# Neighbourhood attention outputs by features: values held in TensorE, divided probabilities moving, two heads on two column halves

## The chip, the cores and the metric

One core of one Trainium2 chip runs the whole program. The metric is the device time of one execution in microseconds (us), as a median over several runs; lower is better.

## What is computed

A trunk of two layers over 256 tokens of width 1024, all in float32. Each layer is a mixer, a cross attention and a gated convolutional feed-forward. The change touches the mixer, which joins three groups of heads: six mLSTM heads (384 columns), five heads of 2-D neighbourhood attention (320 columns) and five heads of gated linear attention (GLA, 320 columns). For the neighbourhood heads, head size 64, this is

```
s = einsum('brqhd,brkwhd->bhrqkw', qg, k_band) * (d ** -0.5) + bias
s = where(in_win, s, -inf)
p = softmax(s)                        # over all keys of a query
o = einsum('bhrqkw,brkwhd->brqhd', p, v_band)
...
mixed = concatenate([ml_out, na_out, gla_out], axis=-1)
return mixed @ w_out
```

The grid is 4 rows of 64 columns, so that every query sees all 4 rows; the window in the columns is a mask in `bias`. Hence p is, for each head, a full 256 x 256 matrix.

## The kernel before

Every engine runs an order written out by hand, and engines wait for each other on semaphores that count finished jobs. TensorE (PE) multiplies; ScalarE (ACT) and VectorE (DVE) empty its banks of PSUM. A product with weights is made of three matmuls in fp32r: the weights come by DMA as `raw`, ACT makes `whi`, their rounded high part (L1096), and DVE makes `wlo`, the rest (L1455); activations are split the same way (`yhi`, `ylo`). A unit of weights (xk0, xv0a, wo0b ...) can be used once its low part is made. `split_lo(unit)` in DVE's order makes all low parts up to that unit.

The neighbourhood stage is the loop `for hh in range(NAH + 2)`, once in each engine's code. Its jobs for head g are:

- `nas{g}` (L882): scores on PE, two heads together, at hh = 0, 2 and 4. DVE subtracts bias and keeps the extreme (L1624), ACT makes the exponential into `np_` and its row sums `nsum` (L1262). `np_` has two places, g modulo 2.
- `nat{g}` (L864): four turnings of `np_`, at hh = g + 1; ACT copies them to `npt` (L1249).
- `nao{g}` (L872): the outputs, at hh = g + 2. The turned probabilities are held (128 x 128) and 64 columns of values `nav` move. DVE takes the reciprocal of `nsum` (L1611) and multiplies the outputs by it into `tmb` (L1614).

In between PE has fill work: halves (24 matmuls) of the units xk0 to xk3 of the cross attention, two halves at hh = 1, 2 and 3 and one at hh = 4 and 5 in layer 0; in layer 1 one half of 24 at hh = 1, 2 and 3, then 18 matmuls and 6. DVE has other work in the loop too: the low parts of the weights, the sums of the mLSTM heads, the gated queries and keys of GLA (L1646, L1647, at hh = 2), their decayed form (L1655, at hh = 3) and the squares of the mLSTM heads (L1588, `head_squares`). After the loop PE turns GLA keys, `kt0` (L900), into bank 5 and goes on with GLA.

When all three groups of heads are in `tmb`, PE turns its eight blocks of 128 columns (16 turnings, L978, `mx`), ACT writes `yhi` (L1301), DVE writes `ylo` (L1710), and PE multiplies by the output weights, units wo0a, wo0b, wo1a and wo1b. Blocks 3 and 4 and the first half of block 5 belong to the neighbourhood heads.

Of the kernel before, what the change touches and what calls it, by code (L numbers as in the profile page):

```python
# [21 lines left out]
P = 128  # L22
# [90 lines left out]
def layer_events(l):  # L113
# [43 lines left out]
    for h in range(NAH + 2):  # L157
        if 1 <= h <= NAH:
            job(f"nat{h - 1}", 2 + (h - 1) % 2)
        if h >= 2:  # L160
            job(f"nao{h - 2}", 4 + (h - 2) % 2)
        if h < NAH and h % 2 == 0:
            for n in range(h, min(h + 2, NAH)):
                job(f"nas{n}", n % 2)
        if h == 0:
            tm("gg", (7, 6))
        for i in NA_FILL[l][h]:
            if i % 2:
                job(f"xk{i // 2}", (7, 6)[i // 2 % 2], f"xk{i // 2}")
# [48 lines left out]
def layer_drains(l):  # L218
# [15 lines left out]
    for h in range(NAH + 2):  # L234
# [5 lines left out]
        if h >= 2:  # L240
            v.append(f"nao{h - 2}")
        if h < NAH and h % 2 == 0:
            v += [f"nas{n}" for n in range(h, min(h + 2, NAH))]
    v += ["kt0", "kt1"]
# [47 lines left out]
def build(nc, a, out):  # L292
    with ExitStack() as ctx:
# [31 lines left out]

        fhi = sb("fhi", [P, 2, 2, T], F32R)
        flo = sb("flo", [P, 2, 2, T], F32R)
        sb("early_rest", [P, T])
        with ExitStack() as mixer:
# [5 lines left out]
            eg = mixer.enter_context(nc.sbuf_tensor("eg", [P, TT, GV], F32))  # L335

# [139 lines left out]
        np_ready = sem("np_ready")  # L476
        zb_ready = sem("zb_ready")
# [45 lines left out]
        def mixed_parts(k):  # L523

            lo, hi = k * P, k * P + P
            return [(slice(max(lo, a) - lo, min(hi, b) - lo), v)
                    for a, b, v in ((0, ML, forwards), (ML, ML + NA, backwards), (ML + NA, DM, forwards)) if max(lo, a) < min(hi, b)]
# [110 lines left out]
        def _(pe):  # L638
# [10 lines left out]
            for l in range(DEPTH):  # L649
# [64 lines left out]
                def tm_half(unit, half, names, n, group, fresh=False, tokens=(0, 1), ks=range(4)):  # L714
                    have((l, unit + half))
                    hi, lo = weights((l, unit + half), 4)
                    x = PAIR[group]
                    for t in tokens:
                        if half == "a":
                            free(names[t])  # L720
                        for k in ks:
                            kk = 4 * "ab".index(half) + k
                            if fresh and t == 0:
                                lo_is(pe, l, group, kk)
                            s = slice(t * P, t * P + P)
                            way = from_the_end if unit in ("xv1", "xw1") and t == TT - 1 and kk == KT - 1 else (lambda v: v)
                            last = split_mm(way(bank(names[t])[:, 0:n]), x[0][:, kk, s], x[1][:, kk, s],
                                            way(hi[:, k, :]), way(lo[:, k, :]), kk == 0, kk == KT - 1)
                        if (half == "b" or t == TT - 1) and k == 3:
# [127 lines left out]
                for hh in range(NAH + 2):  # L857
                    if 1 <= hh <= NAH:
                        g = hh - 1
                        pe.wait_ge(np_ready, NAH * l + g + 1)  # L860
                        free(f"nat{g}")
                        for t in range(TT):
                            for jt in range(TT):
                                last = nc.tensor.transpose(bank(f"nat{g}", TT, TT, P)[:, t, jt, :], np_[:, g % 2, t, jt * P:(jt + 1) * P], ident[:])  # L864
                        last.then_inc(te_done, 1)
# [194 lines left out]
        def _(act):  # L1060
# [44 lines left out]
            for l in range(DEPTH):  # L1105
# [140 lines left out]
                for hh in range(NAH + 2):  # L1246
                    if 1 <= hh <= NAH:
# [48 lines left out]
                for k in range(KT):  # L1296
                    is_filled(act, l, f"mx_{k % 4}")
                    if k >= 4:
                        lo_is(act, l, "mx", k - 4)
                    for r, v in mixed_parts(k):  # L1300
                        last = A(forwards(yhi[r, k, :]), v(turned_bank(l, "mx", k)[r, :]), ACT.Copy, scale=pcol[r, R_MG + k:R_MG + k + 1])  # L1301
                    last.then_inc(xhi_ready, 1)
# [115 lines left out]
        def _(dve):  # L1418
# [39 lines left out]
            for l in range(DEPTH):  # L1458
# [145 lines left out]

                for hh in range(NAH + 2):
                    if hh == 2:
                        dve.wait_ge(eb_ready, 2 * l + 2)
                    if hh >= 2:
                        g = hh - 2
                        dve.wait_ge(np_ready, NAH * l + g + 1)  # L1610
                        link(V.reciprocal(nsum[:, 2 * g:2 * g + 2], nsum[:, 2 * g:2 * g + 2]))  # L1611
                        is_filled(dve, l, f"nao{g}")
                        for t in range(TT):
                            last = ts(tmb[:, t, ML + g * DH:ML + (g + 1) * DH], bank(f"nao{g}")[:, t * DH:(t + 1) * DH],  # L1614
                                      nsum[:, 2 * g + t:2 * g + t + 1], None, ALU.mult)
                        drain(last)
# [10 lines left out]
                    if hh == 0:  # L1627
                        split_lo("ggb")
# [260 lines left out]
```

## Time and profile before

| | |
|---|---|
| median of 3 runs | 880.57 us |
| lowest, highest | 878.48, 882.46 us |
| profiled execution | 878.24 us |
| its span from first to last instruction | 876.3 us |
| PE, DVE, ACT busy | 861.8, 596.0, 496.1 us |
| granted TensorE clock, mean | 0.998 |

The busy times are of the same span, and engines work side by side, so that they do not add up. A share of 98% on PE says that most of the time is its work; it does not say what a wait in one stage would cost. Every time below is of the profiled execution.

### The profile page before, as it was taken

The numbers are of one execution on the slowest core, as the hardware profiler recorded it, in microseconds if no ns is written. First come the engines' busy times: TensorE is split into PE (matmuls) and PEld (weight loads), VectorE is DVE, ScalarE is ACT, GpSimd is POOL, SyncE is SP. The second block draws the span as 40 slices with busy tenths as digits, with TensorE's granted clock in tenths as the row PEclk, the third lists the DMA queues.
The fourth block names the chain that finished last, engine by engine and source line by source line (L and its number), as shares of the span: only waits on it lengthen the run. The fifth ranks groups of instructions, "written<-read, shape, count | busy, mean of one in ns | idle before, by whom it ended". The sixth has DMA issues, their size and how long they took to land.

```text
span 876.3 us, 14948 instructions
## 1 busy us (share of the span) xinstructions
PE 861.8 (98%) x6338; PEld 798.1 (91%) x6338; DVE 596.0 (68%) x820; ACT 496.1 (57%) x689; POOL 14.3 (2%) x35
## 2 busy tenths in 40 slices
PE   8999999999999999999999999999999899999997
PEld 8999998889889999999999999988898899999996
DVE  6887678757657666666577885887665666656655
ACT  7954663658647445445567546745755645445444
POOL 5000000000000000000000000000000000000000
PEclk9999999999999999999999999999999999999999
DMA  9735452364255555555448254335435365555541
GB/s 329 201 102 177 156 178 103 112 226 144 97 193 190 195 190 195 192 191 194 145 140 257 72 171 165 127 115 192 135 109 191 127 212 190 193 196 190 192 169 48
DMA packets 114665, 146.78 MB, mean 168 GB/s; under 512 B 10600, under 2 KB 94760, under 8 KB 114600
## 3 DMA queue, kind: packets, MB, share of 16 engines
q1 hardware_dynamic: 114456, 145.57, 49.7%
q8 instruction: 50, 0.82, 0.4%
q10 hardware_dynamic: 144, 0.26, 0.1%
q14 instruction: 15, 0.12, 0.0%
HBM read 144.77 MB, written 1.05 MB: 166 GB/s over the span
## 4 chain that ended last, share of the span: by engine, by line
PE 92%; ACT 3%; DVE 3%; issue 1%; DMA 0%; ACTq 0%; DVEq 0%
PE bank L665 26%; PE bank L666 25%; PE bank L667 25%; PE bank L706 4%; PE bank L743 2%; PE bank L832 2%; DVE wlo L1455 2%; PE bank L1017 2%; ACT whi L1096 1%; ACT yhi L1119 1%; PE bank L872 1%; PE bank L762 1%; PE bank L849 1%; DVE ylo L1710 1%; PE bank L882 1%
## 5 line engine op out<-in xcount | busy, mean ns | idle before, releaser
L1455 DVE TENSOR_TENSOR wlo<-raw,whi 128x2048 fp32r<-128x2048 f32 (+3 forms) x144 | 306.2, 2133 | 106.1 <-ACT whi L1096 105.2
L1096 ACT ACTIVATE whi<-raw 128x2048 fp32r<-128x2048 f32 (+3 forms) x144 | 257.4, 1793 | 53.5 <-PE bank L667 48.4
L665 PE MATMUL bank<-yhi,whi 128*128 128x256 f32 x704 | 195.1, 277 | 0.5 <-DVE ylo L1471 0.5
L666 PE MATMUL bank<-ylo,whi 128*128 128x256 f32 x704 | 194.6, 276 | 0.0
L667 PE MATMUL bank<-yhi,wlo 128*128 128x256 f32 x704 | 194.6, 276 | 0.0
L665 PEld LDWEIGHTS bank<-yhi,whi 128*128 128x128 f32 x704 | 132.2, 188 | 1.6 <-issue 0.7
L666 PEld LDWEIGHTS bank<-ylo,whi 128*128 128x128 f32 x704 | 132.2, 188 | 0.8
L667 PEld LDWEIGHTS bank<-yhi,wlo 128*128 128x128 f32 x704 | 132.2, 188 | 0.0
L665 PE MATMUL bank<-xhi,whi 128*128 128x256 f32 x320 | 91.4, 286 | 2.2 <-DVE wlo L1455 1.2
L665 PE MATMUL bank<-whi,xhi 128*128 128x512 f32 (+2 forms) x256 | 90.1, 352 | 0.0
L667 PE MATMUL bank<-xhi,wlo 128*128 128x256 f32 x320 | 88.9, 278 | 0.0
L666 PE MATMUL bank<-xlo,whi 128*128 128x256 f32 x320 | 88.8, 278 | 0.0
L667 PE MATMUL bank<-whi,xlo 128*128 128x512 f32 (+2 forms) x256 | 88.5, 346 | 0.0
L666 PE MATMUL bank<-wlo,xhi 128*128 128x512 f32 (+2 forms) x256 | 88.5, 346 | 0.0
L666 PE MATMUL bank<-wlo,fhi 128*128 128x512 f32 x176 | 69.0, 392 | 0.0
L665 PE MATMUL bank<-whi,fhi 128*128 128x512 f32 x176 | 68.9, 391 | 0.0
L667 PE MATMUL bank<-whi,flo 128*128 128x512 f32 x176 | 68.6, 390 | 0.0
L665 PEld LDWEIGHTS bank<-xhi,whi 128*128 128x128 f32 x320 | 60.3, 188 | 7.1 <-issue 5.2
L1395 ACT ACTIVATE arena<-bank,pcols 128x256 f32<-128x256 f32 x44 | 22.4, 561 | 67.1 <-PE bank L667 67.1
L667 PEld LDWEIGHTS bank<-xhi,wlo 128*128 128x128 f32 x320 | 60.1, 188 | 0.0
L666 PEld LDWEIGHTS bank<-xlo,whi 128*128 128x128 f32 x320 | 60.1, 188 | 0.0
L665 PEld LDWEIGHTS bank<-whi,xhi 128*128 128x128 f32 x256 | 48.1, 188 | 5.1 <-issue 1.3
(268 smaller groups left out, 1373.1 us busy)
## 6 DMA issues: line engine op xcount, KB each, us to landing
raw<-in_w_up SPq DMA_DIRECT2D x44, 1024.0 KB, 5.0
raw<-in_w_down SPq DMA_DIRECT2D x22, 1024.0 KB, 4.8
raw<-in_w_in SPq DMA_DIRECT2D x10, 1024.0 KB, 7.3
raw<-in_w_xk SPq DMA_DIRECT2D x8, 1024.0 KB, 5.1
raw<-in_w_xv SPq DMA_DIRECT2D x8, 1024.0 KB, 4.9
raw<-in_w_out SPq DMA_DIRECT2D x8, 1024.0 KB, 4.8
raw<-in_w_xq SPq DMA_DIRECT2D x8, 1024.0 KB, 5.7
raw<-in_w_xo SPq DMA_DIRECT2D x8, 1024.0 KB, 4.9
```

What stands on the lines that cost most here:

```text
L665: mm(o, s_hi, m_hi, start=first, stop=False, skip_group_check=True)
L666: mm(o, s_hi, m_lo, start=False, stop=False, skip_group_check=True)
L667: return mm(o, s_lo, m_hi, start=False, stop=last, skip_group_check=True)
L706: last = mm(bank(name, 2, T)[:, f, :], w[:, k, f * P:f * P + P], x[:, k, :], start=k + i + f == 0, stop=k == KT - 1 and i == 2, skip_group ...
L743: last = mm(bank(names[t])[:, 0:n], x[:, k, t * P:(t + 1) * P], w[:, k, :], start=k + i == 0, stop=False, skip_group_check=True)
L762: last = nc.tensor.transpose(turned_bank(l, group, k)[:, t * P:(t + 1) * P], tmb[:, t, k * P:(k + 1) * P], ident[:])
L832: last = mm(o[:, t, d, :], w[:, c:c + P], mv[:, jt, g, :], start=i == 0, stop=i == len(src) - 1)
L849: last = mm(bank(f"mls{hh + x}", TT, T)[:, jt, :], qk[r, 3 + j, jt * P:(jt + 1) * P], qk[r, j, :], start=True, stop=True)
L1017: last = mm(bank(f"xo_{hh}", 2, T)[:, f, :], xv[:, jt, hh * XD + f * P:hh * XD + (f + 1) * P], xpt[:, hh, jt, :], start=jt == 0, stop=jt == 1)
L1096: A(weight(whi, gu), raw[:, gu % RING, 0:SIZE[gu]], ACT.Copy).then_inc(hi_done, 1)
L1395: last = A(fy[:, p % 2, f, :], bank(f"fa{p}", 2, T)[:, f, :], ACT.Identity, scale=pcol[:, RA + RB_W + 22 + j:RA + RB_W + 23 + j], bias=pco ...
L1455: tt(weight(wlo, gu), raw[:, gu % RING, 0:SIZE[gu]], weight(whi, gu), ALU.subtract).then_inc(lo_done, 1)
```

## The change

PE now makes the outputs with the values held (128 tokens x 64 features of one head) and the turned probabilities of all 256 queries moving. Of a pair of heads, one writes partitions 0 to 63 and the other 64 to 127 of the same bank. The three groups (heads 0 and 1, 2 and 3, and 4) are made at hh = 3, 5 and 6. What comes out has features on the partitions, which is what the output product needs, so blocks 3, 4 and half of 5 are no longer turned: ACT writes their high part `yna_hi` straight from the bank, and DVE their low part `yna_lo` (`heads_lo`). The row sums can't be divided out of such outputs by a factor per partition, so DVE divides `np_` by them before PE turns it (`shares_of`), and PE's turning waits for that (`npn_ready`) instead of for the exponential. The output product starts with block 3.

```diff
     for h in range(NAH + 2):
+        if h in NA_OUT:
+            p = NA_OUT.index(h)
+            job(f"nao{p}", 4 + p % 2)
...
-        if h >= 2:
-            job(f"nao{h - 2}", 4 + (h - 2) % 2)
...
+NA_OUT = (3, 5, 6)
+NA_PAIRS = ((0, 1), (2, 3), (4,))
+NA_K = range(3, 6)
...
+        def mixed(k):
+
+            r = slice(64, P) if k == 5 else slice(0, P)
+            return (r,) + tuple(x[r] for x in operand("mx", k))
+
+        MIXED_K = (0, 1, 2, 5, 6, 7)
...
                 for hh in range(NAH + 2):
+                    if hh in NA_OUT:
+                        p = NA_OUT.index(hh)
+                        is_drained(pe, l, f"nat{NA_PAIRS[p][-1]}")
+                        free(f"nao{p}")
+                        for jt in range(TT):
+                            for g in NA_PAIRS[p]:
+                                r = slice(64 * (g % 2), 64 * (g % 2) + 64)
+                                last = mm(bank(f"nao{p}")[r, 0:T], nav[:, jt, g * DH:(g + 1) * DH], npt[:, g % 2, jt].rearrange("p a b -> p (a b)"),
+                                          start=jt == 0, stop=jt == 1, skip_group_check=True)
+                        last.then_inc(te_done, 1)
                     if 1 <= hh <= NAH:
                         g = hh - 1
-                        pe.wait_ge(np_ready, NAH * l + g + 1)
+                        pe.wait_ge(npn_ready, NAH * l + g + 1)
...
-                    if hh >= 2:
-                        g = hh - 2
-                        is_drained(pe, l, f"nat{g}")
-                        free(f"nao{g}")
-                        for t in range(TT):
-                            for jt in range(TT):
-                                last = mm(bank(f"nao{g}")[:, t * DH:(t + 1) * DH], npt[:, g % 2, t, jt, :],
-                                          nav[:, jt, g * DH:(g + 1) * DH], start=jt == 0, stop=jt == 1)
...
                     for k in (i, i + 4):
+                        if k not in MIXED_K:
+                            continue
...
-                for n in range(2):
-                    tm_unit(f"wo{n}", (f"wo{n}0", f"wo{n}1"), 512, "mx", n == 0)
+                tm_half("wo0", "a", ("wo00", "wo01"), 512, "mx", True, ks=(3,), first=3, ends=None)
+                tm_half("wo0", "a", ("wo00", "wo01"), 512, "mx", True, ks=(0, 1, 2), first=3, ends=2)
+                tm_half("wo0", "b", ("wo00", "wo01"), 512, "mx", True)
+                tm_unit("wo1", ("wo10", "wo11"), 512, "mx")
...
                 for hh in range(NAH + 2):
+                    if hh in NA_OUT:
+                        p = NA_OUT.index(hh)
+                        r = slice(0, 64 * len(NA_PAIRS[p]))
+                        is_filled(act, l, f"nao{p}")
+                        A(forwards(yna_hi[r, p, :]), backwards(bank(f"nao{p}")[r, 0:T]), ACT.Copy).then_inc(na_hi_ready, 1)
...
+                def shares_of(g):
+                    dve.wait_ge(np_ready, NAH * l + g + 1)
+                    link(V.reciprocal(nsum[:, 2 * g:2 * g + 2], nsum[:, 2 * g:2 * g + 2]))
+                    for t in range(TT):
+                        last = ts(np_[:, g % 2, t, :], np_[:, g % 2, t, :], nsum[:, 2 * g + t:2 * g + t + 1], None, ALU.mult)
+                    last.then_inc(npn_ready, 1)
+
+                def heads_lo(p):
+                    dve.wait_ge(na_hi_ready, 3 * l + p + 1)
+                    r = slice(0, 64 * len(NA_PAIRS[p]))
+                    drain(tt(forwards(yna_lo[r, p, :]), backwards(bank(f"nao{p}")[r, 0:T]), forwards(yna_hi[r, p, :]), ALU.subtract))
...
-                    if hh >= 2:
-                        g = hh - 2
-                        dve.wait_ge(np_ready, NAH * l + g + 1)
-                        link(V.reciprocal(nsum[:, 2 * g:2 * g + 2], nsum[:, 2 * g:2 * g + 2]))
-                        is_filled(dve, l, f"nao{g}")
...
                     if hh == 0:
                         split_lo("ggb")
+                        for g in NA_PAIRS[0]:
+                            shares_of(g)
...
                         if l == 0:
                             split_lo("xk2")
+                        for g in NA_PAIRS[1]:
+                            shares_of(g)
...
                         if l == 0:
                             split_lo("xk3")
+                        heads_lo(0)
...
                     if hh == 4:
                         split_lo("xv0a")
-                    if hh == 5 and l:
-                        head_squares(mlh, sq, 0, MLH)
+                        shares_of(4)
+                    if hh == 5:
+                        if l:
+                            head_squares(mlh, sq, 0, MLH)
+                        heads_lo(1)
...
+                heads_lo(2)
```

What moves is seen best in each engine's own order. First DVE, layer 1, at hh = 2, between the reductions of heads 2 and 3 and the decayed keys; this is before the change, where `wlo` is the low part of xk3:

```order
L1624 ISA nmax 128x1
L1455 TENSOR_TENSOR wlo<-raw,whi 128x2048
L1646 TENSOR_TENSOR arena<-gq,arena 128x512
L1647 TENSOR_TENSOR arena<-gk,arena 128x512
L1646 TENSOR_TENSOR arena<-gq,arena 128x512
L1647 TENSOR_TENSOR arena<-gk,arena 128x512
L1611 RECIPROCAL nsum<-nsum 128x2
L1614 TENSOR_SCALAR tmb<-bank,nsum 128x64 x2
L1655 TENSOR_TENSOR arena<-arena 128x512 x2
```

and the same place of the changed kernel:

```order
L1661 ISA nmax 128x1
L1489 TENSOR_TENSOR wlo<-raw,whi 128x2048
L1685 TENSOR_TENSOR arena<-gq,arena 128x512
L1686 TENSOR_TENSOR arena<-gk,arena 128x512
L1685 TENSOR_TENSOR arena<-gq,arena 128x512
L1686 TENSOR_TENSOR arena<-gk,arena 128x512
L1641 RECIPROCAL nsum<-nsum 128x2
L1643 TENSOR_SCALAR arena<-arena,nsum 128x256 x2
L1641 RECIPROCAL nsum<-nsum 128x2
L1643 TENSOR_SCALAR arena<-arena,nsum 128x256 x2
L1696 TENSOR_TENSOR arena<-arena 128x512 x2
```

The reciprocal at this place was for head 1's outputs; now those of heads 2 and 3 stand here, with the division of the probabilities (in `arena`), behind xk3's low part and the four products of GLA.

Second PE, layer 1, around head 2's turning, at hh = 3. Before, behind the last matmuls of xk2:

```order
L665 MATMUL bank<-xhi,whi 128x256
L666 MATMUL bank<-xlo,whi 128x256
L667 MATMUL bank<-xhi,wlo 128x256
L864 MATMUL bank<-ident,arena 128x128 x4
L872 MATMUL bank<-nav,arena 128x64 x4
```

and after:

```order
L684 MATMUL bank<-xhi,whi 128x256
L685 MATMUL bank<-xlo,whi 128x256
L686 MATMUL bank<-xhi,wlo 128x256
L890 MATMUL bank<-arena,nav 64x256 x4
L899 MATMUL bank<-ident,arena 128x128 x4
```

The outputs of heads 0 and 1 now stand ahead of head 2's turning (L899), where those of head 1 stood behind it.

Third DVE, layer 0, at hh = 4 and 5, behind head 4's reductions. Before:

```order
L1624 ISA nmax 128x1
L1588 TENSOR_TENSOR qk<-qk 128x768
L1589 TENSOR_REDUCE hs<-qk 128x12
L1455 TENSOR_TENSOR wlo<-raw,whi 128x2048
L1611 RECIPROCAL nsum<-nsum 128x2
L1614 TENSOR_SCALAR tmb<-bank,nsum 128x64 x2
```

and after:

```order
L1661 ISA nmax 128x1
L1622 TENSOR_TENSOR qk<-qk 128x768
L1623 TENSOR_REDUCE hs<-qk 128x12
L1489 TENSOR_TENSOR wlo<-raw,whi 128x2048
L1641 RECIPROCAL nsum<-nsum 128x2
L1643 TENSOR_SCALAR arena<-arena,nsum 128x256 x2
L1649 TENSOR_TENSOR yna_lo<-bank,yna_hi 128x256
```

Head 4's division, for which its turning on PE now waits, stands behind the squares and the low part of xv0a.

## Rows read from the trace of the kernel before

**Rows 1.** The page: PE's busy time, and the last chain by engine.

```profile
PE 861.8 (98%) x6338; PEld 798.1 (91%) x6338; DVE 596.0 (68%) x820; ACT 496.1 (57%) x689; POOL 14.3 (2%) x35
...
PE 92%; ACT 3%; DVE 3%; issue 1%; DMA 0%; ACTq 0%; DVEq 0%
```

**Rows 2.** Timeline of DVE, layer 1: start, duration, line, names, count, idle before.

```profile
553.40 0.17 DVE L1611 RECIPROCAL nsum<-nsum 128x2 f32<-128x2 f32 x1 [0.83 <-ACT arena L1257]
...
554.00 0.41 DVE L1624 CUSTOM_DVE_ANT_0 arena<-bank,bt 128x256 f32<-128x256 f32 x1
...
555.38 2.29 DVE L1455 TENSOR_TENSOR wlo<-raw,whi 128x2048 fp32r<-128x2048 f32 x1
...
560.10 0.17 DVE L1611 RECIPROCAL nsum<-nsum 128x2 f32<-128x2 f32 x1
```

**Rows 3.** Timeline of PE, layer 1, from head 2's turning to kt0.

```profile
555.95 0.66 PE L864 MATMUL bank<-ident,arena 128*128 128x128 f32 x4
...
557.81 0.35 PE L665 MATMUL bank<-xhi,whi 128*128 128x256 f32 x1 [0.36 <-DVE wlo L1455]
...
560.72 0.60 PE L864 MATMUL bank<-ident,arena 128*128 128x128 f32 x4
...
568.18 0.61 PE L900 MATMUL bank<-ident,arena 128*128 128x128 f32 x4
```

**Rows 4.** The chain in layer 0: start, time on the chain, records.

```profile
128.97 0.44 PE bank L864 x4
129.41 0.84 PE bank L872 x8
130.25 1.06 PE bank L882 x4
...
152.35 1.45 PE bank L956 x12
```

**Rows 5.** Timeline of PE, layer 0, mixer turnings and wo0a.

```profile
165.00 1.91 PE L978 MATMUL bank<-ident,tmb 128*128 128x128 f32 x16
166.77 0.47 PE L665 MATMUL bank<-whi,yhi 128*128 128x512 f32 x1
...
172.09 0.39 PE L667 MATMUL bank<-whi,ylo 128*128 128x512 f32 x1
172.79 0.50 PE L665 MATMUL bank<-whi,yhi 128*128 128x512 f32 x1 [0.32 <-DVE wlo L1455]
```

**Rows 6.** Timeline of DVE in the same stretch.

```profile
166.14 2.19 DVE L1710 SCALAR_TENSOR_TENSOR ylo<-bank,pcols,yhi 128x256 fp32r<-128x256 f32 x5 [0.45 <-ACT yhi L1301]
...
170.46 6.68 DVE L1455 TENSOR_TENSOR wlo<-raw,whi 128x2048 fp32r<-128x2048 f32 x3
```

**Rows 7.** Timeline of DVE, layer 0, a division in the cross attention.

```profile
217.70 0.62 DVE L1746 TENSOR_SCALAR tmb<-tmb,nsum 128x256 f32<-128x256 f32 x2
```

**Rows 8.** Timeline of DVE, layer 0, in the neighbourhood stage.

```profile
105.34 2.29 DVE L1455 TENSOR_TENSOR wlo<-raw,whi 128x2048 fp32r<-128x2048 f32 x1 [1.26 <-ACT whi L1096]
...
113.50 2.29 DVE L1455 TENSOR_TENSOR wlo<-raw,whi 128x2048 fp32r<-128x2048 f32 x1
...
132.04 0.95 DVE L1588 TENSOR_TENSOR qk<-qk 128x768 f32<-128x768 f32 x1
...
133.90 2.28 DVE L1455 TENSOR_TENSOR wlo<-raw,whi 128x2048 fp32r<-128x2048 f32 x1
```

**Rows 9.** Timeline of PE, layer 0, head 4's turning and kt0.

```profile
134.18 0.60 PE L864 MATMUL bank<-ident,arena 128*128 128x128 f32 x4
...
139.09 0.61 PE L900 MATMUL bank<-ident,arena 128*128 128x128 f32 x4
```

**Rows 10.** Windows at the end: stretch, its length, busy of PE to POOL, PEclk, DMA share, GB/s.

```profile
870.00:871.00 1.00, 0.34 (x2) 0.00 (x0) 0.97 (x3) 0.80 (x3) 0.00 (x0) 1.00 0.00 0
...
873.00:874.00 1.00, 0.00 (x0) 0.00 (x0) 0.20 (x1) 0.17 (x1) 0.00 (x0) 0.82 0.02 6
874.00:875.00 1.00, 0.00 (x0) 0.00 (x0) 0.00 (x0) 0.00 (x0) 0.00 (x0) 0.50 0.96 375
```

More of the change, by code:

```diff
@@ L324, in build @@
             xql = early.enter_context(nc.sbuf_tensor("xql", [P, KT * T + HALF], F32R))
+        with ExitStack() as early:
+            early.enter_context(nc.sbuf_tensor("queries_keys", [P, 6 * T], F32))
+            yna_hi = early.enter_context(nc.sbuf_tensor("yna_hi", [P, 3, T], F32R))
         fhi = sb("fhi", [P, 2, 2, T], F32R)
@@ L335, in build @@
             eg = mixer.enter_context(nc.sbuf_tensor("eg", [P, TT, GV], F32))
+        with ExitStack() as mixer:
+            yna_lo = mixer.enter_context(nc.sbuf_tensor("yna_lo", [P, 3, T], F32R))
         chi = sb("chi", [P, KT, T], F32R)
@@ L521, in forwards, with operand @@
             return v.rearrange("p (r c) -> p r c", c=GW)
[L523 to L527, printed above, removed]
+        def operand(group, k):
+            if group == "mx" and k in NA_K:
+                return yna_hi[:, k - 3, :], yna_lo[:, k - 3, :]
+            return tuple(x[:, k, :] for x in PAIR[group])
+        def mixed(k):
+            r = slice(64, P) if k == 5 else slice(0, P)
+            return (r,) + tuple(x[r] for x in operand("mx", k))
+        MIXED_K = (0, 1, 2, 5, 6, 7)
         block = ctx.enter_context(nc.Block())
@@ L712, in fm_unit, with input_is, tm_half @@
                     fm_blocks(name, group, [(f, 0, KT) for f in range(WCOLS[UNIT[l, name]] // P)], fresh, stepped=stepped)
-                def tm_half(unit, half, names, n, group, fresh=False, tokens=(0, 1), ks=range(4)):
+                def input_is(group, kk):
+                    if group == "mx" and kk in NA_K:
+                        is_drained(pe, l, f"nao{kk - 3}")
+                    if group != "mx" or kk in MIXED_K:
+                        lo_is(pe, l, group, kk)
+                def tm_half(unit, half, names, n, group, fresh=False, tokens=(0, 1), ks=range(4), first=0, ends=3):
                     have((l, unit + half))
                     hi, lo = weights((l, unit + half), 4)
-                    x = PAIR[group]
                     for t in tokens:
-                        if half == "a":
+                        if half == "a" and ks[0] == first:
                             free(names[t])
@@ L723, in tm_half @@
                             if fresh and t == 0:
-                                lo_is(pe, l, group, kk)
+                                input_is(group, kk)
                             s = slice(t * P, t * P + P)
+                            x = operand(group, kk)
                             way = from_the_end if unit in ("xv1", "xw1") and t == TT - 1 and kk == KT - 1 else (lambda v: v)
-                            last = split_mm(way(bank(names[t])[:, 0:n]), x[0][:, kk, s], x[1][:, kk, s],
-                                            way(hi[:, k, :]), way(lo[:, k, :]), kk == 0, kk == KT - 1)
-                        if (half == "b" or t == TT - 1) and k == 3:
+                            last = split_mm(way(bank(names[t])[:, 0:n]), x[0][:, s], x[1][:, s],
+                                            way(hi[:, k, :]), way(lo[:, k, :]), kk == first, kk == KT - 1)
+                        if (half == "b" or t == TT - 1) and k == ends:
                             last.then_inc(te_done, 1)
@@ L863, in _ @@
                             for jt in range(TT):
[L864 to L873 removed]
+                                last = nc.tensor.transpose(bank(f"nat{g}", TT, TT, P)[:, jt, t, :], np_[:, g % 2, t, jt * P:(jt + 1) * P], ident[:])
                         last.then_inc(te_done, 1)
@@ L1295, in _ @@
                 split_hi("wo0b")
-                for k in range(KT):
+                for k in MIXED_K:
                     is_filled(act, l, f"mx_{k % 4}")
-                    if k >= 4:
+                    if k - 4 in MIXED_K:
                         lo_is(act, l, "mx", k - 4)
-                    for r, v in mixed_parts(k):
-                        last = A(forwards(yhi[r, k, :]), v(turned_bank(l, "mx", k)[r, :]), ACT.Copy, scale=pcol[r, R_MG + k:R_MG + k + 1])
-                    last.then_inc(xhi_ready, 1)
+                    r, hi, _ = mixed(k)
+                    A(hi, turned_bank(l, "mx", k)[r, :], ACT.Copy, scale=pcol[r, R_MG + k:R_MG + k + 1]).then_inc(xhi_ready, 3 if k == 5 else 1)
                 split_hi("wo1b")
@@ L1706, in _ @@
                 split_lo("wo0a")
-                for k in range(KT):
+                for k in MIXED_K:
                     hi_is(dve, l, "mx", k)
-                    for r, v in mixed_parts(k):
-                        last = stt(forwards(ylo[r, k, :]), v(turned_bank(l, "mx", k)[r, :]), pcol[r, R_MG + k:R_MG + k + 1],
-                                   forwards(yhi[r, k, :]), ALU.mult, ALU.subtract)
-                    last.then_inc(xlo_ready, 1)
+                    r, hi, lo = mixed(k)
+                    stt(lo, turned_bank(l, "mx", k)[r, :], pcol[r, R_MG + k:R_MG + k + 1], hi, ALU.mult, ALU.subtract
+                        ).then_inc(xlo_ready, 3 if k == 5 else 1)
                 split_lo("wo1b")
```

12 lines of the change are left out of this document (5 added, 7 removed).

## The prediction

> **What bounds the kernel now.** I read the page first: TensorE (PE) is busy 861.8 of 876.3 us, and of the chain that ended last it holds 92%, VectorE (DVE) and ScalarE (ACT) 3% each [rows 1]. So a microsecond of PE work is worth a microsecond, unless PE is made to wait. Then the stage that the change touches, as DVE and as PE see it (the timelines). In layer 1 DVE is behind there: it leaves a wait for ACT at 553.40, evacuates head 0 and reduces heads 2 and 3 from 554.00, makes the low part of xk3 from 555.38, multiplies the gated queries and keys, and only at 560.10 comes to the next head's sums [rows 2]. PE has begun to turn head 2 at 555.95 and waits a mere 0.36 us, for xk3 at 557.81 [rows 3]. DVE's lateness costs little now, because what PE needs from it stands early in DVE's queue.
>
> **What it removes and adds on PE.** Before, one head's outputs are 8 records in 0.84 us (4 matmuls, an fp32 matmul being two records) [rows 4]; five heads, 4.20 us a layer. After, a pair of heads is 4 matmuls with 64 columns held and 256 moving. No such product stands in the trace; the nearest row has its shape: 12 records of 128 rows by 64 columns with 256 moving, going to alternate column halves, in 1.45 us [rows 4]. A record of 256 columns is 0.213 us, if the four records of nas4 in 1.06 us have 0.2 of run-in [rows 4]; twelve in a line would be 2.56, six rounds of two are 1.28, with 0.17 over. So there two halves run side by side, and a pair here is 4 rounds, 0.85, and 0.2: 1.06. The fifth head alone is 4 records, again 1.06. Three groups are 3.18 a layer: **1.02 saved**. The dear end is 8 records in a line, 1.9 a pair; a gain beyond rounds of two is excluded, since there are two halves.
>
> Four of the 16 mixer turnings go. Sixteen take from 165.00 to 166.77, 0.11 each [rows 5]: **0.44 saved** a layer. The low parts there are fewer too: DVE makes nine pieces from 166.14 and starts the low part of wo0b at 170.46 [rows 6]; PE, whose last matmul of wo0a starts at 172.09 and could be followed 0.23 later, starts the next at 172.79 [rows 5]: 0.47 lost. After, six pieces are two thirds of 4.32, 2.88, and begin 0.22 sooner, as two turnings and not four stand ahead of the first: from the stage's start 1.14 - 0.22 + 2.88 + 2.20 for the low part + 0.14 hand-over = 6.1 us, while PE has 1.33 of turnings and 24 matmuls at 0.2275, 6.8 us. The wait goes, since k = 3 needs no turning and can go first: **0.46 saved**. Layer 1 repeats it. Together 0.9 a layer in this stage.
>
> **What it moves.** The division was made on outputs, behind PE's turning and product. It now stands ahead of the turning, and PE's nat of each head waits for it. It is a reciprocal (0.17 busy, 0.19 to the next start [rows 2]) and two multiplications over 128x256, of which a pair takes 0.62 us in the cross attention [rows 7]: 0.81, and 0.14 to hand over (the low part of xk3 ends at 557.67, PE starts at 557.81 [rows 2, 3]). ACT's three new copies and DVE's three subtractions a layer take the place of three of nine pieces each in the mixer turning, so about even, and they stand where DVE and ACT have PE's fill units as cover; uncovered they would be 0.4 each. Divisions 0 and 1 are early: they fill a wait of DVE for ACT of 1.26 us [rows 8] with some 1.5, and push what is behind by 0.25. The other three are not early.
>
> *Layer 1.* DVE leaves 553.40 as before. Then four reductions (554.00 to 555.38), 1.38; low part of xk3 and the multiplications (555.38 to 560.10), 4.72; division 2, 0.81; hand-over 0.14. Sum 7.05: nat2 starts at **560.45**. PE is there at 555.95 - 0.84 + 1.06 = 556.2 and waits **4.2 us**; behind nat2 are queued xk3's first half, nat3, nas4 and the stage's rest, and DVE waits for nas4. From 560.45: nat2 0.44 [rows 4], first half 2.91 (557.81 to 560.72 [rows 3]), nat3 0.44, nas4 1.06: DVE gets head 4 at 565.3. Two reductions 0.69, the low part of xv0a 2.20, division 4 0.81, hand-overs 0.18: nat4 at 569.2. PE, with 18 matmuls (2.18) and the second pair (1.06), is there at 568.5 and waits 0.7. Then 0.44, six matmuls 0.73, outputs of head 4 1.06: kt0 at 571.4. Before, 568.18 [rows 3]. **+3.2.** What is late next is the release of kt0's bank (behind division 4 the head squares, 1.86, and a subtraction, 0.4), also 571.4.
>
> *Layer 0.* xk1 cannot start before its low part, which ends at 115.79 [rows 8] and is now 0.25 later, so the first output group that goes gains nothing. From there to nas4 two groups of 0.84 go and one of 1.06 comes: nas4, which ends at 131.31 [rows 4], ends at 130.7. DVE then has two reductions 0.69, head squares 1.86 (132.04 to 133.90 [rows 8]), the low part of xv0a 2.20, division 4 0.81, hand-overs 0.18: nat4 at 136.4, not 134.18 [rows 9], with PE waiting 1.8 us. Then 0.44, half a unit 2.9, outputs 1.06: kt0 at 140.8, against 139.09 [rows 9]. **+1.7.** Head 2's division is made by 123 here, about when PE comes: a wait of 0.2 or 0.3 at most.
>
> Behind kt0 DVE is less late than before, so the last head's subtraction fits. All later stages are PE's own and shift with it.
>
> **Sum.** +1.7 + 3.2 - 0.9 - 0.9 = +3.1 us, against the profiled execution's own 878.24: 881.3. That one lies 2.3 under the median 880.57, to which the same +3.1 gives **883.7** (+0.36%).
>
> **Rivals.**
> *The clock falls in the wait.* 4.2 us would be PE's longest pause but the last. In that one PE ends at 870.3; the granted clock is 1.00 in 870 to 871, 0.82 in 873 to 874 and 0.50, the 1.2 GHz level, in 874 to 875 [rows 10]. So it fell some 3.3 us after PE's end, sooner than 4.2. If it falls here, PE works at half rate until the clock is back; nat2 to the end of nas4 is 4.85 us, which bounds the loss in this stretch. It may be back at once, hence 0 to 4.9; I take 2, since no row shows the return. Time 885.7, and it is slower by over 0.5% from 1.3 us on. Against it: the pause is hardly longer than the one row. Chance 0.22. The Trainium skill (TensorE: Matmul & The Clock Gate, "Why this matters for your kernels") has as a rule that idle gaps between bursts of matmuls send the clock back to half. By that rule, the trace's end agrees.
> *The waits do not come*, the divided values being there in time: faster than before. Place: nat2 of layer 1; it decides if division 2 is done by 556.1. Then the savings alone stay: 2 x (1.02 + 0.9) = 3.8, 876.7, near the bound of 0.5%. For it speaks how few waits PE has now; against it that the groups of rows 2 up to 560.10 stand ahead of division 2 in program order. Chance 0.07.
> *Column halves do not run side by side.* A pair is 1.9. In layer 1 the first pair is under the wait; the second pairs are under the waits at nat4 but for 0.15; in layer 0 the first is on the path. +1.0: 884.7. Against it the row of 1.45. Chance 0.05.
>
> **How the numbers follow.** My forecast, waits at full clock, has 0.62; its own range is 882.2 to 885.2: some 0.3 either way for each of the four chains, and a median that moves by about 1 (runs from 878.48 to 882.46). Anything else has 0.04. What can't be told from no change is 0.5%, 4.4 us: 876.2 to 885.0. Slower by more: a sixth of the forecast (0.10), three quarters of the clock (0.17), half of the halves and the rest (0.04): 0.31. Faster: a third of the second rival and a little of the rest, 0.04. Same 0.65. For 8 in 10 the range goes from 880.8, under the forecast's own, to 887.2, inside the clock's case.
>
> **What would show it.** After: PE idle some 4 us ahead of nat2 in layer 1, released by the division on DVE; 1.5 to 2 us ahead of nat4 in layer 0, under 1 in layer 1; pairs of about 1.05 us; 12 turnings in about 1.3; no idle at wo0b; a granted clock of 1.00 behind the wait, or 0.5 if the rival holds. I am wrong if DVE reaches division 2 much before 559, if a new wait of PE is elsewhere (kt0, kv), or if the clock falls.

## The result, and the profile after

| | before | after |
|---|---|---|
| median of 6 runs | 879.81 us | 884.84 us |
| lowest, highest | 878.48, 882.46 us | 883.76, 885.55 us |
| after by before | | 1.0054 [1.0037, 1.0071] |
| profiled execution, its span | 878.24, 876.3 us | 883.83, 881.8 us |
| PE, DVE, ACT busy | 861.8, 596.0, 496.1 us | 860.7, 597.3, 496.0 us |

The change made the kernel 5.0 us slower, 0.54%, with 3.3 to 6.2 us inside the interval. The forecast was +3.1 and 883.7 us. The prediction took 0.5% as what can't be told from no change: 1.0054 is just beyond that, and the interval reaches to both sides of it.

The page of the changed kernel, the lines that answer to [rows 1]:

```profile
PE 860.7 (98%) x6290; PEld 793.4 (90%) x6290; DVE 597.3 (68%) x820; ACT 496.0 (56%) x689; POOL 14.3 (2%) x35
...
PE 90%; DVE 5%; ACT 3%; issue 1%; DMA 0%; ACTq 0%; DVEq 0%
```

PE has 48 records less and its busy time fell by only 1.1 us, although the change takes more work than that away: some of what is left ran slower. DVE's busy time rose by 1.3 us, but its share of the last chain from 3% to 5%: in more places than before the end now hangs on DVE's queue. The view of all waits names the one that is new among PE's (engine, line, what was waited for: total, times, longest):

```profile
PE bank L899 <- DVE arena L1643: 6.4, 3, 4.2
```

Line 899 is the turning of the probabilities, L1643 the division. No wait for the exponential stood at this place before. The timeline of PE in layer 1, answering to [rows 3]:

```profile
556.27 1.08 PE L890 MATMUL bank<-arena,nav 128*64 128x256 f32 x8
561.52 0.72 PE L899 MATMUL bank<-ident,arena 128*128 128x128 f32 x4 [4.16 <-DVE arena L1643]
561.93 0.52 PE L684 MATMUL bank<-xhi,whi 128*128 128x256 f32 x1
562.25 0.41 PE L685 MATMUL bank<-xlo,whi 128*128 128x256 f32 x1
...
565.23 0.36 PE L684 MATMUL bank<-xhi,whi 128*128 128x256 f32 x1
565.43 0.28 PE L685 MATMUL bank<-xlo,whi 128*128 128x256 f32 x1
...
566.35 0.60 PE L899 MATMUL bank<-ident,arena 128*128 128x128 f32 x4
...
571.81 0.66 PE L899 MATMUL bank<-ident,arena 128*128 128x128 f32 x4 [0.53 <-DVE arena L1643]
573.15 1.08 PE L890 MATMUL bank<-arena,nav 128*64 128x256 f32 x4
574.16 0.66 PE L926 MATMUL bank<-ident,arena 128*128 128x128 f32 x4
```

The first pair of outputs (L890) is made at 556.27, then PE stands still for 4.16 us until head 2's division ends. Behind the wait the matmuls of xk3 have records of 0.41 us that follow each other at 0.213 until 565.23, and then 0.28 at 0.117: for 3.3 us PE runs at about half its rate. The windows of one microsecond in the same stretch show why (the last three numbers are the granted clock, the DMA share and GB/s):

```profile
557.00:558.00 1.00, 0.35 (x4) 0.00 (x0) 1.00 (x1) 1.00 (x3) 0.00 (x0) 1.00 0.00 0
...
560.00:561.00 1.00, 0.00 (x0) 0.00 (x0) 0.93 (x4) 0.00 (x0) 0.00 (x0) 1.00 0.94 336
561.00:562.00 1.00, 0.48 (x5) 0.48 (x5) 0.96 (x5) 0.00 (x0) 0.00 (x0) 0.99 1.03 401
562.00:563.00 1.00, 1.00 (x7) 1.00 (x6) 1.00 (x3) 0.60 (x1) 0.00 (x0) 0.50 0.65 250
...
564.00:565.00 1.00, 1.00 (x6) 1.00 (x6) 0.00 (x0) 0.00 (x0) 0.00 (x0) 0.50 0.00 0
565.00:566.00 1.00, 1.00 (x9) 1.00 (x8) 0.00 (x0) 0.00 (x0) 0.00 (x0) 0.80 0.00 0
566.00:567.00 1.00, 1.00 (x10) 0.83 (x9) 0.00 (x0) 0.01 (x1) 0.00 (x0) 1.00 0.00 0
```

The clock stays at 1.00 during the whole pause and falls to 0.50, the 1.2 GHz level, just after PE has begun to work again, until about 565.4. That is this one profile; in two other kernels with the same wait the clock fell already during the pause (halves_in_line below).

DVE at the same place, answering to [rows 2]:

```profile
554.54 0.42 DVE L1661 CUSTOM_DVE_ANT_0 arena<-bank,bt 128x256 f32<-128x256 f32 x1 [0.65 <-ACT arena L1292]
...
555.92 2.29 DVE L1489 TENSOR_TENSOR wlo<-raw,whi 128x2048 fp32r<-128x2048 f32 x1
558.12 0.69 DVE L1685 TENSOR_TENSOR arena<-gq,arena 128x512 f32<-128x512 f32 x1
...
560.65 0.17 DVE L1641 RECIPROCAL nsum<-nsum 128x2 f32<-128x2 f32 x1
560.85 0.62 DVE L1643 TENSOR_SCALAR arena<-arena,nsum 128x256 f32<-128x256 f32 x2
```

While PE waits, DVE makes xk3's low part, which PE does not need before the turning, and four products for GLA, which it needs more than 10 us later. In layer 0 the timeline of PE shows the wait of head 4, then the outputs of head 4 and `kt0`, answering to [rows 9], and the start of the output product, answering to [rows 5]:

```profile
122.05 1.08 PE L890 MATMUL bank<-arena,nav 128*64 128x256 f32 x8
123.06 0.66 PE L899 MATMUL bank<-ident,arena 128*128 128x128 f32 x4
...
136.53 0.66 PE L899 MATMUL bank<-ident,arena 128*128 128x128 f32 x4 [1.71 <-DVE arena L1643]
139.87 1.08 PE L890 MATMUL bank<-arena,nav 128*64 128x256 f32 x4
140.87 0.66 PE L926 MATMUL bank<-ident,arena 128*128 128x128 f32 x4
...
166.84 1.47 PE L1006 MATMUL bank<-ident,tmb 128*128 128x128 f32 x12
168.06 0.48 PE L684 MATMUL bank<-whi,yna_hi 128*128 128x512 f32 x1
```

**Where the 5 us are.** Four starts on the last chain cut each layer at the same work in both kernels: the first scores (nas0), `kt0`, the first turning of the mixer, and the first turning of the next stage. The chain of waits gives (us, before and after):

| stretch | before | after | difference |
|---|---|---|---|
| layer 0, nas0 to kt0 | 39.93 | 41.56 | +1.63 |
| layer 1, nas0 to kt0 | 29.89 | 34.69 | +4.80 |
| kt0 to the mixer's turnings, layers 0 and 1 | 25.91, 25.91 | 26.06, 26.04 | +0.15, +0.13 |
| mixer's turnings to the next turning, layer 0 | 27.02 | 25.84 | -1.18 |
| the same, layer 1 | 27.00 | 25.85 | -1.15 |

Together +4.4. The +0.15 and +0.13 of the third row are the turning of `kt0` itself, which now stands behind outputs: 0.59 us on the chain, 0.45 and 0.44 before. The two profiled executions differ by 5.6; 1.2 of it lies in stretches whose work is the same in both kernels, and no run here says more of it.

### The profile page after: what moved, and what is told of

The parts are those of the page before. It is cut to its first block, busy times and chain, and to the rows that moved or that the text cites. A ratio compares the mean times of both kernels' runs of the same rounds, so it can differ in the third digit from the quotient of the medians.

```text
span 881.8 us, 14840 instructions
## 1 busy us (share of the span) xinstructions
PE 860.7 (98%) x6290; PEld 793.4 (90%) x6290; DVE 597.3 (68%) x820; ACT 496.0 (56%) x689; POOL 14.3 (2%) x35
## 4 chain that ended last, share of the span: by engine, by line
PE 90%; DVE 5%; ACT 3%; issue 1%; DMA 0%; ACTq 0%; DVEq 0%
PE bank L684 25%; PE bank L685 24%; PE bank L686 24%; PE bank L725 4%; PE bank L768 2%; DVE wlo L1489 2%; PE bank L857 2%; PE bank L1047 2%; ACT whi L1126 1%; ACT yhi L1149 1%; PE bank L874 1%; PE bank L787 1%; PE bank L991 1%; DVE arena L1661 0%; PE bank L908 0%
```

## The experiments

The theory was: the slowing is the place of the divisions in DVE's order, with the clock's fall on top; the products by features and the four turnings that go are a gain of 3 to 4 us that the waits eat. Rivals: the clock is a bystander; or the products are dearer than the rows suggest. All kernels but before_12_turnings are edits of the changed kernel. Each ratio is against the kernel before on the same chip (879.67 us in 33 runs for the first four, 879.42 in 26 for the other four).

**no_division.** The division is left out, so the probabilities stay undivided; PE's turning waits for the exponential again.

```diff
                 def shares_of(g):
-                    dve.wait_ge(np_ready, NAH * l + g + 1)
-                    link(V.reciprocal(nsum[:, 2 * g:2 * g + 2], nsum[:, 2 * g:2 * g + 2]))
-                    for t in range(TT):
-                        last = ts(np_[:, g % 2, t, :], np_[:, g % 2, t, :], nsum[:, 2 * g + t:2 * g + t + 1], None, ALU.mult)
-                    last.then_inc(npn_ready, 1)
+                    return
...
-                        pe.wait_ge(npn_ready, NAH * l + g + 1)
+                        pe.wait_ge(np_ready, NAH * l + g + 1)
```

> The changed kernel without the division: DVE neither takes the reciprocals nor multiplies the probabilities, and PE's turning of each head waits for the exponential, as before the change. The outputs of the neighbourhood heads are therefore not divided by their sums. Theory 1 (the new products and the shorter mixer turning save about 3.8 us, and everything lost comes from turnings that wait for a division that stands late in DVE's queue, with the clock falling in the longest wait): all waits at the turnings are gone, the granted clock stays at 1.00 in layer 1, and the time is 3.5 to 4.5 under the kernel before, 876; ratio 0.995 to 0.996. Theory 2 (the held-values product itself is dear, by switching PE between full width and column halves, and the savings are not there): the time is about that of the kernel before or above it, 879 to 882, ratio 1.00 or more.

Measured 877.51 us, ratio 0.9970 [0.9960, 0.9981]: -2.6 us by the ratio, less than the 3.5 to 4.5 expected. The waits at L899 are gone. By the chain, nas0 to kt0 is 39.62 in layer 0 (-0.31 against before) and 28.91 in layer 1 (-0.98), the mixer 25.84 (-1.18), and +0.15 from kt0 to the mixer: -3.3 over both layers, inside the interval of the whole (-1.7 to -3.5). Everything but the division is thus a gain, a little smaller than the 3.8 forecast.

**div2_early.** In layer 1 head 2 is divided ahead of GLA's products.

```diff
                         if l:
                             split_lo("xk3")
+                            shares_of(2)
                         is_drained(dve, l, "gk")
...
                         for g in NA_PAIRS[1]:
-                            shares_of(g)
+                            if g == 3 or l == 0:
+                                shares_of(g)
```

> One edit to the changed kernel, layer 1 only: head 2's division stands right behind the low part of xk3, ahead of the four GLA products. Theory 1: PE waits about 1.8 us at head 2's turning in layer 1 instead of 4.16 (low part ends at 558.1, division 0.81, hand-over 0.14, PE ready at 557.3), the clock does not fall, the half unit behind it takes 2.9 us and not 4.4; time 2.4 + 1.5 = 3.9 under the changed kernel, 880.9. If the clock's fall had nothing to do with the wait, only 2.4 is gained, 882.4, and the granted clock still falls there. Theory 2: the wait moves to the next turning or to head 4's, and the time falls by under 1 us.

Measured 879.71 us, ratio 0.9998 [0.9988, 1.0007]. One division moved past four products takes back the whole loss. The timeline of PE in layer 1:

```profile
558.85 0.66 PE L899 MATMUL bank<-ident,arena 128*128 128x128 f32 x4 [1.63 <-DVE arena L1643]
559.26 0.36 PE L684 MATMUL bank<-xhi,whi 128*128 128x256 f32 x1
...
562.17 0.60 PE L899 MATMUL bank<-ident,arena 128*128 128x128 f32 x4
```

The wait is 1.63 instead of 4.16 us, and the half unit behind it takes 2.91 (559.26 to 562.17) instead of 4.42 (561.93 to 566.35). The stage is 30.66 instead of 34.69: of the 4.03, 2.53 is the wait and 1.51 the clock. The whole came out 1.2 us better than the 880.9 expected; no stage of the two profiles shows why. The sum took 1.5 us for the clock from one profile, and halves_in_line has 2.1 for the same wait.

**div4_early.** Head 4 is divided ahead of the low part of xv0a (in layer 1 the pair's low part too).

```diff
-                    if hh == 4 and l == 0:
-                        head_squares(mlh, sq, 0, MLH)
                     if hh == 4:
-                        split_lo("xv0a")
+                        head_squares(mlh, sq, 0, MLH)
                         shares_of(4)
-                    if hh == 5:
                         if l:
-                            head_squares(mlh, sq, 0, MLH)
+                            heads_lo(1)
+                        split_lo("xv0a")
+                    if hh == 5 and l == 0:
                         heads_lo(1)
```

> One edit to the changed kernel: head 4's division stands behind the squares of the mLSTM heads (which cover the exponential) and ahead of the low part of xv0a, in both layers; in layer 1 the second pair's low part also moves ahead of xv0a, as kt0's bank waits for it. Theory 1: the waits of 1.71 and 0.53 us at head 4's turning go and nothing takes their place; time 2.0 to 2.2 under the changed kernel, 882.7. The fall of the clock at head 2's turning stays. Theory 2: kt0 or the GLA states wait instead, time unchanged within 0.5.

Measured 882.31 us, ratio 1.0029 [1.0018, 1.0039]. Layer 0 goes from 41.56 to 39.50, and head 4's wait is gone there; in layer 1 0.19 of 0.53 us is left. Head 2's wait is as before the edit:

```profile
PE bank L899 <- DVE arena L1643: 4.4, 2, 4.2
```

**both_early.** Both edits.

> Both moves together. Theory 1: the two add up, 6.0 under the changed kernel, 878.8, which is 1 us under the kernel before: ratio 0.999. What stays is 1.8 us at head 2's turning in layer 1 and 0.3 to 0.4 each at the low parts of layer 0 and 1. Theory 2: less than the sum of the two runs, with a new wait at kt0 or at the GLA products.

Measured 877.28 us, ratio 0.9970 [0.9959, 0.9980], 1.5 us better than expected: the stages are 39.50 and 30.30, about as the two single edits had them, so that they give 6.45 us under the changed kernel, where 6.0 was expected. The other 1.1 us lie in no stage that the profiles show. It is 2.4 us faster than the kernel before, by the ratios 0.8% faster than the changed one, and equal to the kernel without a division, though 1.8 us of waits are left (1.64 at head 2's turning in layer 1, 0.18 at head 4's).

**clock_kept.** In layer 1 PE multiplies idly in head 2's wait: 16 products of the unit matrix, whose result is thrown away by the turning behind them.

```diff
-                        pe.wait_ge(npn_ready, NAH * l + g + 1)
                         free(f"nat{g}")
+                        if l and g == 2:
+                            keep_clock(16, bank(f"nat{g}"))
+                        pe.wait_ge(npn_ready, NAH * l + g + 1)
```

> The changed kernel with 16 matmuls of the identity on itself (fp32, 128 columns), put on PE between the outputs of heads 0 and 1 and the wait of head 2's turning, in layer 1 only; they fill some 3.4 of the 4.16 us wait and change no output. Theory 1 with the clock as a cause of its own: the start of head 2's turning stays where it is, the granted clock stays 1.00, the half unit behind it takes 2.9 us instead of 4.4: 1.5 us faster than the changed kernel in the profile, and 1.5 to 3 in the median, since runs of the changed kernel with a lower mean clock were longer. If the clock is not what made the half unit long: no change.

Measured 882.86 us, ratio 1.0037 [1.0024, 1.0051]. The timeline of PE and the windows:

```profile
559.63 3.84 PE L664 MATMUL bank<-ident 128*128 128x128 f32 x32
563.87 0.66 PE L901 MATMUL bank<-ident,arena 128*128 128x128 f32 x4 [0.40 <-DVE arena L1645]
564.28 0.36 PE L684 MATMUL bank<-xhi,whi 128*128 128x256 f32 x1
...
567.11 0.60 PE L901 MATMUL bank<-ident,arena 128*128 128x128 f32 x4
```

```profile
560.00:563.00 3.00, 3.00 (x30) 3.00 (x29) 2.97 (x6) 2.32 (x3) 0.00 (x0) 1.00 0.35 85
563.00:567.00 4.00, 3.60 (x33) 3.41 (x31) 3.00 (x9) 0.60 (x1) 0.00 (x0) 1.00 0.53 202
```

The division comes no sooner, the clock stays at 1.00, and the half unit takes 2.83 us. The stage is 33.17 instead of 34.69, 1.52 less. The interval of the whole overlaps that of the changed kernel, 1.0054 [1.0037, 1.0071], and touches, at 1.0051, that of the next kernel, run on the same chip, whose wait is the change's own. So the gain of 1.5 us is shown in the stage, and only borne out by the whole.

**halves_in_line.** The four matmuls of a pair in the order of the heads instead of alternating between the column halves.

```diff
-                        for jt in range(TT):
-                            for g in NA_PAIRS[p]:
+                        for g in NA_PAIRS[p]:
+                            for jt in range(TT):
                                 r = slice(64 * (g % 2), 64 * (g % 2) + 64)
```

> The changed kernel with the four matmuls of a pair in another order: both of one head, then both of the other, so that column halves alternate once and not three times. If alternating is what makes two halves run side by side, a pair takes about 1.5 to 1.9 us instead of 1.06; the time rises by 0.5 to 1.0 us, since only the first pair of layer 0 is on PE's path and the others lie under waits. If PE pairs them in any order, or never does, the rows stay at 1.06 and so does the time.

Measured 885.29 us, ratio 1.0066 [1.0051, 1.0081], which overlaps the changed kernel's, and the pair in layer 0 is as long as in the alternating order:

```profile
122.53 1.09 PE L890 MATMUL bank<-arena,nav 128*64 128x256 f32 x8
```

On the chain such a pair is 1.02 us. The theory that alternating makes the halves run side by side falls: written in line they take no longer. That they do run side by side is borne out by the single head, whose four records in one half take the same 1.01 (139.87 to 140.87 above) as the pair's eight in two.

The stage of layer 0 is as long as in the changed kernel (41.62 and 41.56 us), that of layer 1 0.58 longer (35.27). This is the clock. Windows, and then the chain's two turnings around the half unit:

```profile
558.00:562.00 4.00, 0.32 (x4) 0.00 (x0) 3.93 (x7) 2.94 (x5) 0.00 (x0) 0.79 0.38 103
562.00:563.00 1.00, 0.52 (x3) 0.52 (x4) 0.96 (x5) 0.00 (x0) 0.00 (x0) 0.50 1.06 414
...
566.00:570.00 4.00, 4.00 (x25) 3.44 (x25) 0.41 (x3) 0.60 (x1) 0.00 (x0) 0.86 0.00 0
```

```profile
562.48 1.12 PE bank L899 x4
...
568.06 0.44 PE bank L899 x4
```

The wait is 4.16 us again, but the clock falls within it, at about 560.3, 2.2 us before PE begins, and is back at about 567.1. From one turning to the next PE takes 5.58 us, not 4.99 as in the changed kernel, nor 3.48 as at full clock in both_early: here the fall costs 2.1 us. In div4_early PE waits 4.17 us, until 559.58; the fall begins at about 558.9, 0.7 us before, and the stretch takes 4.67 us, a cost of 1.2. Its windows:

```profile
558.00:562.00 4.00, 2.42 (x12) 2.42 (x13) 3.68 (x11) 0.63 (x2) 0.00 (x0) 0.61 0.66 251
```

**before_12_turnings.** The kernel before, without the four turnings of blocks 3 and 4 and their high and low parts; the output product takes blocks 0 and 1 in their stead, so that it has the same matmuls on other data.

```diff
                     for k in (i, i + 4):
+                        if k in (3, 4):
+                            continue
...
-                for k in range(KT):
+                for k in (0, 1, 2, 5, 6, 7):
```

> The kernel before with 12 mixer turnings instead of 16: blocks 3 and 4 are neither turned nor split, and the output product takes blocks 0 and 1 in their place, so that the output is not the reference's. Nothing else of the change is in it. Theory 1: 0.44 us of turnings and the 0.47 us wait at wo0b go in each layer: 1.8 us under the kernel before, ratio 0.998. In the changed kernel's own trace the stretch from the mixer turning to the next normalised tokens was 1.15 us shorter in each layer, so up to 2.3 would do too. Theory 2: under 1 us, the wait at wo0b staying.

Measured 878.43 us, ratio 0.9991 [0.9981, 1.0001]; the mixer's stage is 26.26 in layer 0 and 26.27 in layer 1, -0.76 and -0.73. So of the change's 1.18, some 0.75 come from the turnings and pieces that go. Some 0.4 are left for what this kernel has not: block 3 first, which needs no turning, and the neighbourhood half of block 5, whose pieces are made from the bank of the outputs. No run takes these two apart. (Block 5 itself is still turned whole, for its other half: the twelve turnings are six blocks.)

**more_early.** both_early, and head 1's division, the wait for GLA's gates and a sum of the mLSTM heads moved too.

```diff
-                    if hh == 2:
-                        dve.wait_ge(eb_ready, 2 * l + 2)
...
-                        for g in NA_PAIRS[0]:
-                            shares_of(g)
+                        shares_of(0)
...
                         memory_lo("mem", l, range(KT))
+                        shares_of(1)
-                        link(tt(mlh, hraw[:, :, 0, :, 0:DH], hraw[:, :, 1, :, 0:DH], ALU.add))
...
+                        dve.wait_ge(eb_ready, 2 * l + 2)
...
+                        link(tt(mlh, hraw[:, :, 0, :, 0:DH], hraw[:, :, 1, :, 0:DH], ALU.add))
                         heads_lo(0)
```

> Both moves (division of head 2 behind xk3's low part in layer 1, of head 4 ahead of xv0a) and three more in DVE's order: head 1's division stands behind the low parts of the memory, the last sum of the mLSTM heads moves from hh = 0 to hh = 3, and the wait for the decays' exponentials stands at the GLA products that need them instead of ahead of heads 2 and 3's reductions. Theory 1: the waits at the low parts (0.3 to 0.4 in each layer) go, and head 2's turning in layer 1 waits 0.6 us instead of 1.8; time 2 us under the kernel with both moves, 876.9, which is 3 under the kernel before: ratio 0.9965. Theory 2: no less than the kernel with both moves.

Measured 876.98 us, ratio 0.9973 [0.9963, 0.9983]: not to be told from both_early. The stages are 39.36 and 30.04, 0.4 us shorter in all, less than the whole can show. Head 2's turning in layer 1 waits 0.64 us, as expected, but head 4's now waits 0.75, where it was 0.18: more than half of what one turning gains the other loses.

## Why the prediction came out as it did

**What bounds the kernel.** Right. A microsecond that PE waits is a microsecond of the end: 2.53 us of wait and 1.51 of clock made 4.03 in div2_early's stage.

**Layer 1, the wait.** Right in place and size. The stage starts 1.09 us later in the profile after (nas0 at 539.54, not 538.45). With that taken off, head 2's turning starts at 560.43, forecast 560.45; the wait is 4.16, forecast 4.2. What let it be read to a tenth is that DVE works there without a gap: its queue could be added up row by row.

**Layer 1, the clock.** This is the step that failed: the forecast's own case held the wait at full clock (0.62) and put the fall at nothing; as a rival it had 0.22, with a price of 2 us. By the prediction's own sign ("or if the clock falls") its case was wrong. The clock fell, and cost 1.5 us (the half unit took 4.42, not 2.91; clock_kept took back 1.52). It was no accident of one profile: all three profiles with this wait show a fall, at 1.5, 1.2 (div4_early) and 2.1 us (halves_in_line), so that the rival's 2 us was a fair price. The mean granted clock of the six runs of the changed kernel is 0.993 to 0.997, of the twelve with div4_early 0.993 to 0.997, and of the eleven with div2_early, whose wait is 1.63, 0.996 to 1.000. The argument against the fall was that the pause is hardly longer than the 3.3 us of the end [rows 10]. But that row has the fall sooner than 4.2 us after PE's end, so it spoke for the fall; it should have been the likelier case, and the sum then 4.6 with the 1.5 measured, or 5.1 with the prediction's 2, around the 5.0 of the medians. The Trainium skill (TensorE: Matmul & The Clock Gate, "Why this matters for your kernels") has idle gaps between bursts send the clock back to half: the traces agree, at 4.16 and 4.17 us, and do not show it at 1.63.

**Head 4.** Its turning was forecast at 136.4 in layer 0 and starts at 136.53 after 1.71 us (1.8); in layer 1 it waits 0.53 (0.7). With the shift and the clock's 1.5 taken off, 571.81 is 569.2, as forecast. `kt0` comes at 140.94 on the chain (140.8) and, by the same subtraction, 571.6 (571.4). The sum of layer 0 left out the 0.25 that it had itself found for xk1's low part: nas4 ends at 130.88, not at the 130.7 of the sum.

**The outputs.** The group of 1.06 us is 1.01 to 1.02 in layer 0 (in layer 1 head 4's is 1.06), so the saving of 1.02 a layer would be 1.15 there; but the turning behind a group takes 0.59 on the chain (0.58 to 0.59 for all three in layer 0 of no_division), where it took 0.44 [rows 4]. That is 0.15 three times a layer, which the sum did not have: net 0.7. In no_division a turning with no outputs ahead of it still takes 0.44 (131.06), so it goes with the outputs. The Trainium skill (TensorEngine Tiling, "Key Properties") says that a change of the tiling mode drains the engine; by that rule, the 0.15 is the drain, and the trace agrees with the place, though no run here took it apart. In layer 0 most of the gain is under the low part of xk1 besides, as forecast: no_division shows -0.31 there and -0.98 in layer 1.

**The mixer.** Forecast -0.9 a layer, measured -1.18 and -1.15, with its parts: the twelve turnings take 1.22 us from start to the first product (168.06 less 166.84), where 1.33 was forecast and sixteen took 1.77, and the wait at wo0b is gone.

**The sum.** +1.7 in layer 0 was +1.63 and 0.15; +3.2 in layer 1 was +3.3 and 0.13 and the clock's 1.5; -1.8 was -2.3. That is +4.4, and the rest up to the median's +5.0 is within the interval. That the time ended inside the forecast's own range, 882.2 to 885.2, is in part luck. Two terms missed in opposite directions, clock and switches up by 1.8, mixer down by 0.5. And the range was laid from a median of 880.57, that of the three runs then known; with six runs the kernel before has 879.81. As a difference the range was +1.6 to +4.6, and the measured +5.0 lies outside it. Of the two times named, the clock's 885.7 is a little nearer to 884.84 than the forecast's 883.7.

**The rivals.** The clock did fall. The column halves do run side by side. That the waits do not come was wrong as the change stands, but its time, 876.7, is what the change is worth once two divisions are moved: 877.28.

## What to carry to other kernels

When an operation moves from behind PE's work to ahead of it, add up the queue of the engine that makes it from the last point where that engine waits; if nothing PE needs sooner stands in that queue, move the operation ahead of it. Here two divisions in another place turn +0.5% into -0.3%, and the change's own arithmetic was never the trouble. And price a wait of PE of about 4 us with the half clock behind it: three profiles of three show it, at 1.2 to 2.1 us. Look at the windows in the wait and after it, since the fall began 2.2 and 0.7 us before PE's next work in two of them and 0.5 after its start in the third.

## What the runs showed of the hardware

**The clock falls without a pause, in some executions.** In five of the ten profiles (no_division, both_early, clock_kept, before_12_turnings, more_early) the clock is at half for some 3.4 us, from a start between 28.4 and 29.4 us, in the other five at 1.00, with the same work of PE. In both_early's:

```profile
26.00:29.00 3.00, 3.00 (x16) 2.02 (x14) 2.96 (x7) 1.64 (x6) 0.00 (x0) 1.00 0.33 69
29.00:30.00 1.00, 1.00 (x9) 1.00 (x8) 0.97 (x3) 1.00 (x3) 0.00 (x0) 0.69 1.03 384
30.00:31.00 1.00, 1.00 (x7) 1.00 (x7) 0.72 (x1) 1.00 (x1) 0.00 (x0) 0.50 0.85 245
...
32.00:33.00 1.00, 1.00 (x8) 1.00 (x7) 1.00 (x1) 0.98 (x2) 0.00 (x0) 0.60 1.16 255
```

The timeline of PE shows no wait ahead of it, but 3 us of small matmuls:

```profile
25.59 0.64 PE L809 MATMUL bank<-gsb,perm 24*64 24x256 f32 x2
26.07 0.59 PE L810 MATMUL bank<-gsb,perm 24*64 24x256 f32 x2
26.59 1.99 PE L818 MATMUL bank<-gaT,w 32*128 32x256 f32 x8
```

They use 24 and 32 of the 128 rows. The kernel before has them too, and its profile shows the clock at 1.00 behind them. Whether they are the cause was not tried. In the five with the fall nas0 starts at 100.98 to 101.66, in the five without at 99.32 to 99.88, at least a microsecond sooner. Such falls may be much of what looks like noise: of the 59 runs of the kernel before beside the experiments, the 17 with a mean clock of 0.996 or less took 880.7 us on average, the 31 with 0.998 or more 879.0. A mean does not say where the clock fell, so that this is not shown. The profiled execution after, with 0.997, is a microsecond under its median, and four of its six runs have 0.995 or less.

**The fall in a wait, and the return.** Three profiles have the same wait of PE, 4.16 or 4.17 us, and three courses of the clock. In the changed kernel it fell 0.5 us after PE's next work had begun and was back some 3.4 us later, with PE busy all the while. In div4_early it fell 0.7 us before, and was also back after some 3.4. In halves_in_line it fell 2.2 us before, and was at half for 6.8. The costs were 1.5, 1.2 and 2.1 us. The bound of 4.9 in the prediction, half rate through nas4, was too high: the matmuls of xk3 follow each other at 0.213 us instead of 0.117, and the clock was back before nas4 in all three.

**Column halves.** Two fp32 matmul chains in the two halves of 64 columns, 8 records of 256 columns, take 1.01 to 1.02 us in layer 0 in either order of writing, one chain of 4 records 1.01.
